# Weight matrices laid out tile by tile in HBM, in a two-block network of 256 tokens

## The chip, the cores and the metric

The kernel runs on one core of a Trainium2 chip. Its time is the device time of one execution in microseconds (us); lower is better. Everything is float32. Weights and inputs lie in HBM (the chip's memory) and reach SBUF (the core's working memory, 128 partitions) by DMA, over 16 DMA engines that all queues of the core share. The kernel's host part is numpy code that arranges the inputs as HBM tensors; it runs before the launch and is not in the time.

## The reference

256 tokens of width 1024 go through two blocks, each of two layers.

```python
# first block, layer i (i = 0: SSD mixer, i = 1: pooling mixer); m, mc come from ada_w, ada_b
x = x + 0.5 * m[:, 2] * swiglu(modulate(x, ...), ffn_w_gate[i, 0], ffn_w_up[i, 0], ffn_w_down[i, 0])
h = h + 0.5 * mc[2] * swiglu(modulate(h, ...), ...)          # context, layer 0 alone
x = x + m[:, 5] * mixer(u, uc)[0]
x = x + 0.5 * m[:, 8] * swiglu(modulate(x, ...), ffn_w_gate[i, 1], ffn_w_up[i, 1], ffn_w_down[i, 1])

# second block, layer l
proj = h @ w_in                                  # attention, short convolution, spatial gating
x = x + g1 * (merged @ w_out)
q = (t @ w_pq).reshape(T, 8, 2, 128)             # expert layer, 8 heads
s = einsum('thpk,hpnk->thpn', q, sub_keys)       # top 16 of 128, twice; then top 16 of 256 pairs
act = gelu(einsum('td,thkd->thk', t, expert_down[experts]))
x = x + g2 * einsum('thk,thkd->td', softmax(best) * act, expert_up[experts])
```

Each token picks 8 x 16 = 128 of 16384 experts, each with a row of 1024 numbers in `expert_down` and one in `expert_up`.

## The kernel before, in words

Each engine has its own instruction stream, written by hand and kept in step by semaphores; each stream runs in order. In the profile PE is TensorE, DVE VectorE, ACT ScalarE, POOL GpSimd and SP the engine that only issues DMAs.

**Weights.** SP loads the weights one tile of 128 x 2048 numbers (1 MB) after another into a ring in SBUF: `wring` with 6 slots in the first block (`load`, line 522), `wring2` with 4 slots in the second (`load2`, line 587); the profile calls both `wring`. A load waits until the tile that had its slot is used up (`weights_consumed`, `weights2_used`). The source is a view of the weight matrix as it came. A gate or up tile takes, for each partition, 8 rows of 256 columns, so 8 pieces of 1 KB (`rows_of(w)[:, :, 256 * i:256 * i + 256]`); `w_in2`, `w_out2`, `peer_wq` and `ssd_w_in` tiles are the same. A down tile or an `ada_w0` tile takes 2 pieces of 4 KB, an `ssd_w_out` tile 16 pieces of 512 B, a `keys` tile (a quarter of a tile) one piece of 2 KB.

**First block.** Five feed-forward parts (`ffn0` to `ffn4`) of 33 tiles each. Each matrix product is made of three passes over a high and a low part of the weights; ACT makes the high part of a tile (`whigh`), DVE the low one (`wlow`). Beside them POOL loads `ada_t` tiles (line 2215, 2 pieces of 4 KB a partition, 3 slots), which DVE multiplies and sums in `condition` (line 1574); there are 112 of them. At the very start 8 tiles of `ada_w0` are multiplied on PE, and DVE turns to their result (line 1458) only behind the low parts of the first three `ffn0` tiles, since it works in order.

**Second block.** It goes through 4 units (2 layers x 2 halves of 128 tokens). A unit has a `mix` (attention, convolution, gating, then the choice of experts) and 128 picks. For pick k POOL gathers, for each of the 128 partitions (tokens), one row of 8 KB (down and up together): 1 MB in all, into one of 8 slots (`rows`, line 2254). DVE multiplies it with the token (line 2125), ACT applies the gelu and makes a diagonal matrix, and PE or DVE adds the up half; then the slot is free. The `mix` of unit u + 1 is woven into the picks of unit u, on each engine at fixed places:

```python
for k in range(PICKS):
    if k >= 2:
        sum_pick(PICKS * unit + k - 2)
    work.go(k)
```

`go(k)` issues those pieces of the mix whose place has come. On PE the 8 `w_in` tiles stand at places 4 to 18, the 4 `w_out` tiles at 35 to 41, the 8 `wq` tiles (`peer_wq`) and 4 `keys` tiles at 48 to 66. So a unit with a mix moves 128 gathers, 20 weight tiles and 4 keys tiles. The mix of unit 0 runs alone, before any pick; unit 3 has no mix beside it. PE waits for its weights in order: while it waits for a tile, its picks wait too.

Of the kernel before, what the change touches and what calls it, by code (L numbers as in the profile page):

```python
# [12 lines left out]
P = 128  # L13
D = 1024
KB = D // P
T = 256
# [3 lines left out]
FFN_ITERS = F // 256  # L20
FFN_TILES = 3 * FFN_ITERS
HIGH_RING = 3
RING = 6
# [14 lines left out]
PH, TOPK, KEYS = 8, 16, 128  # L38
# [31 lines left out]
def consumed(stage, i):  # L70

    return BASE[stage] + i + 1
# [6 lines left out]
ADA_RING = 3  # L79
# [19 lines left out]
RING2 = 4  # L99
# [25 lines left out]
def program(nc, A):  # L125
    ctx = ExitStack()
    with ctx:
        starts = {}

        def sb(name, shape, dt=F32):  # L130
            starts[name] = -(-nc.sbuf_base // 32) * 32
            return ctx.enter_context(nc.sbuf_tensor(name, shape, dt))
# [34 lines left out]
        wring = sb("wring", [P, RING, TILE])  # L167
# [36 lines left out]
        aring = at(2048, ADA_RING, 2, D)  # L204
# [72 lines left out]
        wring2 = second("wring2", [P, RING2, TILE], "wring", 0, RING * TILE)  # L277
# [17 lines left out]
        rows = second("rows", [P, SLOTS, 2 * D], "arena", 3072, AREA)  # L295
# [23 lines left out]
        weights_in = [sem(f"weights_in{i}") for i in range(RING)]  # L319
# [72 lines left out]
        weights2_in = [sem(f"weights2_in{i}") for i in range(RING2)]  # L392
# [119 lines left out]
        @block.sync  # L512
        def _(sp):
            loaded = [0]

            def load(src, a, b):

                n = loaded[0]
                loaded[0] += 1
                if n >= RING:  # L520
                    sp.wait_ge(weights_consumed, n - RING + 1)
                sp.dma_start(wring[:, n % RING, 0:a * b].rearrange("p (a b) -> p a b", a=a), src) \
                    .then_inc(weights_in[n % RING], 16)

            def rows_of(w):
                return w.rearrange("(k p) n -> p k n", p=P)

            def load_columns(w, count, width=256):
                v = rows_of(w)
                for i in range(count):  # L530
                    load(v[:, :, i * width:(i + 1) * width], v.shape[1], width)

            def load_ffn(n, l, f):
                gate_w, up_w, down_w = (rows_of(A[k][l, f]) for k in ("ffn_w_gate", "ffn_w_up", "ffn_w_down"))
                load(gate_w[:, :, 0:256], KB, 256)
                load(up_w[:, :, 0:256], KB, 256)

                load(gate_w[:, :, 256:512], KB, 256)
                load(up_w[:, :, 256:512], KB, 256)
                load(down_w[:, 0:2, :], 2, D)  # L540
                load(gate_w[:, :, 512:768], KB, 256)
                load(up_w[:, :, 512:768], KB, 256)
                load(down_w[:, 2:4, :], 2, D)
                first = loaded[0]
                with sp.Fori(0, (FFN_ITERS - 3) // 2, 1) as it:
                    for j in range(6):
                        slot = (first + j) % RING
                        sp.wait_ge(weights_consumed, it * 6 + (first + j - RING + 1))
                        if j % 3 < 2:
                            src = (gate_w, up_w)[j % 3][:, :, bass.ds(it * 512 + 256 * (3 + j // 3), 256)]  # L550
                            dst = wring[:, slot, :].rearrange("p (a b) -> p a b", a=KB)
                        else:
                            src = down_w[:, bass.ds(it * 4 + 2 * (2 + j // 3), 2), :]
                            dst = wring[:, slot, :].rearrange("p (a b) -> p a b", a=2)
                        sp.dma_start(dst, src).then_inc(weights_in[slot], 16)
                loaded[0] += 6 * ((FFN_ITERS - 3) // 2)
                load(down_w[:, 2 * FFN_ITERS - 2:2 * FFN_ITERS, :], 2, D)

            sp.dma_start(cols[:], A["cols"]).then_inc(cols_in, 16)
            for group in range(2):  # L560
                for i in range(4):
                    load(rows_of(A["ada_w0"])[:, 2 * i:2 * i + 2, group * D:(group + 1) * D], 2, D)
            load_ffn(0, 0, 0)
            load_ffn(1, 0, 0)
            w_ssd = rows_of(A["ssd_w_in"])
            for lat in range(2):
                load(w_ssd[:, :, 5120:5184], KB, 64)
                for i in range(12 if lat else 10):
                    load(w_ssd[:, :, 2048 + 256 * i:2304 + 256 * i], KB, 256)
                for i in range(8 if lat else 0):  # L570
                    load(w_ssd[:, :, 256 * i:256 * i + 256], KB, 256)
            load_columns(A["ssd_w_out"], 8, 128)
            load_ffn(2, 0, 1)
            load_ffn(3, 1, 0)
            load(A["pool_w"].rearrange("g (k p) n -> p (g k) n", p=P), 8, 256)
            load_ffn(4, 1, 1)
            loaded2 = [0]

            def load2(src, a, b):
# [7 lines left out]
                sp.dma_start(wring2[:, n % RING2, 0:a * b].rearrange("p (a b) -> p a b", a=a), src) \  # L587
                    .then_inc(weights2_in[n % RING2], 16)

            for l in range(2):  # L590
                for t in range(TT):
                    for i in W_IN_ORDER:
                        load2(rows_of(A["w_in2"][l])[:, :, 256 * i:256 * i + 256], KB, 256)
                    for i in range(4):
                        load2(rows_of(A["w_out2"][l])[:, :, 256 * i:256 * i + 256], KB, 256)
# [12 lines left out]
            sp.wait_ge(out_stored, 32)  # L608
# [1568 lines left out]
        def _(pool):  # L2177
            g = nc.gpsimd
# [21 lines left out]
            ada = A["ada_t"].rearrange("(b p) k -> p b k", p=P)  # L2200
# [19 lines left out]
            for b in range(NCH * (H // 4) * 2):  # L2220
                c, jb = b // 16, (b // 2) % 8
# [111 lines left out]
```

## Time and profile before

| what | value |
|---|---|
| time, median of 3 runs (lowest to highest) | 3289.71 us (3287.55 to 3296.17) |
| the profiled execution: its own time, its span | 3296.72 us, 3294.7 us |
| PE busy, DVE busy, ACT busy | 80%, 67%, 31% |
| moved by DMA over the span | 976.51 MB in 374436 packets, 260245 of them under 2 KB |
| POOL's queue (q0) | 104848 packets, 656.51 MB |
| SP's queue (q1) | 268304 packets, 312.26 MB |

A packet here is one contiguous piece of a transfer. The span is one execution, from its first to its last instruction; all positions in it are us from its start. The first block ends near 1606 us, the first gather is issued at 1767 us. Units 0, 1 and 2 take their first step behind the opening norm of the mix beside them at 1820.5, 2212.5 and 2605 us; from 2977 us on only picks of unit 3 are left. Times of a wait are idle times of the waiting engine.

### The profile page before, as it was taken

Reading aid. Unit: us, or ns where it says so; the run is one execution under the profiler, and the core shown is the slowest. Engines: PE = TensorE matmul, PEld = TensorE weight load, DVE = VectorE, ACT = ScalarE, POOL = GpSimd, SP = SyncE. Lnnn points to the kernel's source line nnn. Section 1 sums busy time; section 2 is a strip of 40 time slices with the busy share of each in tenths; the row PEclk is TensorE's granted clock in tenths of the full one; section 3 lists DMA queues with packets and bytes.
Section 4 is the critical chain, followed back from the end, with each engine's and each line's share of the span. In section 5 each row is a group of like instructions: output and inputs, shape, how many; then the busy total and the mean of one; then the engine's idle time right before and its main releaser. Section 6 shows DMA issues by size and latency. Waiting matters only on the chain.

```text
span 3294.7 us, 37141 instructions
## 1 busy us (share of the span) xinstructions
PE 2631.4 (80%) x13830; PEld 1990.1 (60%) x13830; DVE 2216.3 (67%) x3855; ACT 1021.6 (31%) x2144; POOL 771.3 (23%) x679
## 2 busy tenths in 40 slices
PE   7999998897699999599873877767766777765566
PEld 4999986686589899599762544235532444321122
DVE  3886865638448868858418666876568765887755
ACT  3433422113134343234322332234222332321222
POOL 0000100004101001001001343443334433445543
PEclk9999998998899999899876989888888888997898
DMA  7777952340159969469536999999999999999998
GB/s 269 271 236 266 367 173 80 105 143 9 39 200 328 333 238 363 146 218 363 184 120 224 401 412 368 417 408 402 405 370 420 402 370 382 398 421 422 422 422 339
DMA packets 374436, 976.51 MB, mean 296 GB/s; under 512 B 17549, under 2 KB 260245, under 8 KB 308256
## 3 DMA queue, kind: packets, MB, share of 16 engines
q0 software_dynamic: 104848, 656.51, 49.5%
q1 hardware_dynamic: 268304, 312.26, 28.7%
q10 hardware_dynamic: 1152, 6.04, 0.5%
q8 instruction: 75, 1.23, 0.2%
q14 instruction: 57, 0.47, 0.0%
HBM read 973.69 MB, written 1.06 MB: 296 GB/s over the span
## 4 chain that ended last, share of the span: by engine, by line
PE 51%; DMA 26%; DVE 13%; ACT 4%; issue 4%; POOL 0%; DVEq 0%; SPq 0%; another core or an unknown queue 0%; ACTq 0%; POOLq 0%
PE psum L624 50%; DMA rows<-in_peer,eidx 17%; DMA wring<-in_peer_wq 4%; DMA wring<-in_w_in 3%; DVE arena L1438 2%; DMA wring<-in_keys 2%; DVE arena L1574 1%; DVE yacc L1441 1%; DVE wlow L1438 1%; PE psum L627 1%; ACT L1060 1%; DVE arena L1444 1%; DVE arena L1441 1%; DVE rows L2125 1%; ACT u L1060 1%
## 5 line engine op out<-in xcount | busy, mean ns | idle before, releaser
L624 PE MATMUL psum<-rows,diag 128*128 128x512 f32 x1392 | 765.9, 693 | 353.5 <-ACT diag L1060 347.5
L2254 POOL DMA_INDIRECT rows<-in_peer,eidx x512 | 636.9, 1244 | 1011.4 <-PE psum L624 665.6
L2125 DVE CUSTOM_DVE_ANT_0 rows<-rows,h2tok 128x1024 f32<-128x1024 f32 x512 | 625.2, 1224 | 282.9 <-DMA rows<-in_peer,eidx 275.7
L624 PEld LDWEIGHTS psum<-rows,diag 128*128 128x128 f32 x1392 | 283.7, 217 | 768.2 <-ACT diag L1060 489.1
L624 PE MATMUL psum<-u_hi,whigh 128*128 128x256 f32 x1760 | 504.3, 287 | 17.7 <-DVE u_lo L1441 14.3
L624 PE MATMUL psum<-u_lo,whigh 128*128 128x256 f32 x1760 | 500.9, 285 | 0.0
L624 PE MATMUL psum<-u_hi,wlow 128*128 128x256 f32 x1760 | 500.8, 285 | 0.0
L1438 DVE TENSOR_TENSOR wlow<-wring,whigh 128x2048 fp32r<-128x2048 f32 x165 | 376.8, 2288 | 164.1 <-ACT whigh L1060 158.0
L1060 ACT ACTIVATE whigh<-wring 128x2048 fp32r<-128x2048 f32 x165 | 314.0, 1908 | 211.8 <-PE psum L624 133.8
L624 PEld LDWEIGHTS psum<-u_hi,whigh 128*128 128x128 f32 x1760 | 340.3, 193 | 21.3 <-issue 15.0
L624 PEld LDWEIGHTS psum<-u_lo,whigh 128*128 128x128 f32 x1760 | 340.9, 194 | 0.0
L624 PEld LDWEIGHTS psum<-u_hi,wlow 128*128 128x128 f32 x1760 | 340.8, 194 | 0.0
L2215 POOL DMA_DIRECT2D arena<-in_ada_t x112 | 80.2, 716 | 1047.0 <-DVE stage L1574 646.6
L624 PE MATMUL psum<-wring,u 128*128 128x256 f32 x1024 | 251.1, 403 | 77.6 <-DMA wring<-in_peer_wq 39.6
L624 PEld LDWEIGHTS psum<-wring,u 128*128 128x128 f32 x1024 | 206.9, 204 | 136.1 <-issue 72.5
L1060 ACT ACTIVATE dots<-dots 128x2 f32<-128x2 f32 x256 | 52.0, 203 | 732.9 <-DVE dots L2125 732.7
L1574 DVE CUSTOM_DVE_ANT_0 arena<-arena 128x1024 f32<-128x1024 f32 x224 | 265.2, 1218 | 10.4 <-DMA arena<-in_ada_t 10.4
L624 PE MATMUL psum<-hid_hi,whigh 128*128 128x256 f32 x880 | 249.3, 283 | 4.7 <-DVE wlow L1438 4.7
L624 PE MATMUL psum<-hid_hi,wlow 128*128 128x256 f32 x880 | 249.0, 283 | 0.0
L624 PE MATMUL psum<-hid_lo,whigh 128*128 128x256 f32 x880 | 249.0, 283 | 0.0
L624 PE MATMUL psum<-u,wring 128*128 128x256 f32 (+1 forms) x992 | 218.9, 382 | 8.4 <-ACT u L1060 7.5
L1441 DVE SCALAR_TENSOR_TENSOR yacc<-rows,dots,yacc 128x1024 f32<-128x1024 f32 x160 | 204.9, 1280 | 28.7 <-ACT dots L1060 28.7
(265 smaller groups left out, 3223.8 us busy)
## 6 DMA issues: line engine op xcount, KB each, us to landing
arena<-in_ada_t POOLq DMA_DIRECT2D x112, 1024.0 KB, 7.4
wring<-in_ffn_w_gate SPq DMA_DIRECT2D x55, 1024.0 KB, 7.1
wring<-in_ffn_w_up SPq DMA_DIRECT2D x55, 1024.0 KB, 7.5
wring<-in_ffn_w_down SPq DMA_DIRECT2D x55, 1024.0 KB, 6.7
wring<-in_w_in SPq DMA_DIRECT2D x32, 1024.0 KB, 19.0
wring<-in_peer_wq SPq DMA_DIRECT2D x32, 1024.0 KB, 16.5
wring<-in_ssd_w_in SPq DMA_DIRECT2D x30, 1024.0 KB, 5.4
wring<-in_w_out SPq DMA_DIRECT2D x16, 1024.0 KB, 19.9
```

The source lines that it names most:

```text
L624: return nc.tensor.matmul(out, lhsT, rhs, start=start, stop=stop, skip_group_check=shared)
L627: return nc.tensor.transpose(out, in_, ident[0:in_.shape[0], 0:in_.shape[0]])
L1060: return nc.scalar.activation(out, in_, fn, **kw)
L1438: return v.tensor_tensor(out, a, b, op)
L1441: return v.scalar_tensor_tensor(out=out, in0=a, scalar=s, in1=b, op0=op0, op1=op1)
L1444: return v.tensor_scalar(out, a, s1, s2, op0, op1) if op1 is not None else v.tensor_scalar(out, a, s1, None, op0)
L1574: ins = v.tensor_tensor_reduce(out=w, in0=w, in1=crow[:, ADA_VECTOR[n], :], scale=1.0, scalar=0.0, op0=ALU.mult, op1=ALU.add, accum_out=st ...
L2125: v.tensor_tensor_reduce(out=rows[:, n % SLOTS, 0:D], in0=rows[:, n % SLOTS, 0:D], in1=h2tok[:, t, :], scale=1.0, scalar=0.0, op0=ALU.mult ...
L2215: pool.dma_start(aring[:, a % ADA_RING], ada[:, 2 * it + 8 * (group + a):2 * it + 8 * (group + a) + 2, :]) \
L2254: pool.indirect_dma_start(out=rows[:, n % SLOTS, :], out_offset=None, in_=A[f"peer{u // 2}"], in_offset=bass.IndirectOffsetOnAxis(ap=eidx[ ...
```

## The change

numpy now writes every weight matrix tile by tile in the order in which the ring takes it, so that a tile is [128, 2048] numbers in HBM with the 8 KB of a partition in one piece, and the whole tile one contiguous megabyte. `load` and `load2` take such a tile as it is; `load_ffn`'s loop picks one by its index. The same holds for POOL's `ada_t` tiles. Each tile in SBUF holds the same numbers at the same places as before, and the number, the order and the queues of the DMAs, all waits and all other engines' instructions stay as they are; the expert tables and the gathers are not touched. A `keys` tile has one piece of 2 KB for each partition before and after.

```diff
-            def load(src, a, b):
+            def load(src):
                 n = loaded[0]
                 loaded[0] += 1
                 if n >= RING:
                     sp.wait_ge(weights_consumed, n - RING + 1)
-                sp.dma_start(wring[:, n % RING, 0:a * b].rearrange("p (a b) -> p a b", a=a), src) \
-                    .then_inc(weights_in[n % RING], 16)
+                sp.dma_start(wring[:, n % RING, 0:src.shape[1]], src).then_inc(weights_in[n % RING], 16)
...
-                load(gate_w[:, :, 0:256], KB, 256)
-                load(up_w[:, :, 0:256], KB, 256)
+                load(gate_w[0])
+                load(up_w[0])
...
-                load(down_w[:, 0:2, :], 2, D)
+                load(down_w[0])
...
-                        load2(rows_of(A["w_in2"][l])[:, :, 256 * i:256 * i + 256], KB, 256)
+                        load2(A["w_in2"][l, i])
...
-                            load2(rows_of(A["peer_wq"][l])[:, :, 256 * head:256 * head + 256], KB, 256)
+                            load2(A["peer_wq"][l, head])
...
-                            load2(A[f"keys{l}"][:, 4 * pair:4 * pair + 4, :], 4, KEYS)
+                            load2(A["keys"][l, pair])
...
-                        pool.dma_start(aring[:, a % ADA_RING], ada[:, 2 * it + 8 * (group + a):2 * it + 8 * (group + a) + 2, :]) \
+                        pool.dma_start(aring[:, a % ADA_RING].rearrange("p a b -> p (a b)"), A["ada_t"][it + 4 * (group + a)]) \
                             .then_inc(ada_in[a], 16)
...
+    def tiles(w, rows, width):
+        lead, (k, n) = w.shape[:-2], w.shape[-2:]
+        w = w.reshape(lead + (k // (rows * P), rows, P, n // width, width))
+        m = len(lead)
+        w = w.transpose(tuple(range(m)) + (m + 3, m, m + 2, m + 1, m + 4))
+        return w.reshape(lead + (n // width * (k // (rows * P)), P, rows * width))
...
-        "ffn_w_gate": I["ffn_w_gate"], "ffn_w_up": I["ffn_w_up"], "ffn_w_down": I["ffn_w_down"],
+        "ffn_w_gate": tiles(I["ffn_w_gate"], KB, 256), "ffn_w_up": tiles(I["ffn_w_up"], KB, 256), "ffn_w_down": tiles(I["ffn_w_down"], 2, D),
...
-        "w_in2": I["w_in_2"], "w_out2": I["w_out_2"], "peer_wq": I["peer_wq_2"],
+        "w_in2": tiles(I["w_in_2"], KB, 256), "w_out2": tiles(I["w_out_2"], KB, 256), "peer_wq": tiles(I["peer_wq_2"], KB, 256),
```

## Rows read from the trace of the kernel before

**Rows 1.** The page: DMA busy tenths and GB/s in 40 slices

```profile
DMA  7777952340159969469536999999999999999998
GB/s 269 271 236 266 367 173 80 105 143 9 39 200 328 333 238 363 146 218 363 184 120 224 401 412 368 417 408 402 405 370 420 402 370 382 398 421 422 422 422 339
```

**Rows 2.** Windows: PE, PEld, DVE, ACT, POOL busy us; clock, DMA share, GB/s

```profile
61.00:447.00 386.00, 383.60 (x3169) 382.90 (x3169) 298.80 (x354) 153.17 (x123) 25.94 (x36) 1.00 0.80 274
...
1820.50:2212.50 392.00, 293.31 (x868) 162.50 (x868) 278.64 (x572) 126.19 (x405) 158.83 (x128) 0.88 1.01 402
2212.50:2605.00 392.50, 286.27 (x840) 158.92 (x840) 277.22 (x573) 124.37 (x405) 152.20 (x129) 0.87 1.01 399
2605.00:2977.00 372.00, 278.52 (x835) 154.47 (x836) 266.05 (x555) 114.00 (x375) 152.08 (x124) 0.90 1.00 394
3020.00:3240.00 220.00, 142.38 (x241) 50.87 (x240) 141.49 (x205) 47.95 (x193) 117.00 (x89) 0.84 1.01 422
```

**Rows 3.** Chain that ended last, unit 0: start us, us, what

```profile
1824.30 25.02 DMA wring<-in_w_in
...
1927.87 36.22 DMA wring<-in_peer_wq
1964.09 19.96 DMA wring<-in_keys
...
1990.07 15.03 DMA wring<-in_keys
...
2013.19 7.33 PE psum L624 x28
```

**Rows 4.** Waits of the whole span: us in total, times, longest

```profile
PE psum L624 <- DMA wring<-in_peer_wq: 39.6, 6, 13.6
...
PE psum L624 <- DMA wring<-in_w_in: 31.2, 4, 14.1
...
PE psum L624 <- DMA wring<-in_keys: 21.7, 4, 9.9
...
DVE arena L1574 <- DMA arena<-in_ada_t: 10.4, 3, 4.7
```

**Rows 5.** DMA queues from 2448 to 2488: packets, MB, share

```profile
q0 software_dynamic: 1998, 14.56, 88.3%
q1 hardware_dynamic: 1875, 1.89, 13.9%
```

**Rows 6.** Windows, columns as in group 2: three short stretches of units 0 and 1

```profile
2248.00:2256.00 8.00, 8.00 (x31) 5.54 (x30) 4.78 (x8) 3.66 (x10) 2.71 (x3) 1.00 1.12 358
2004.00:2020.00 16.00, 14.77 (x53) 10.27 (x54) 8.34 (x21) 3.45 (x13) 3.05 (x3) 0.84 0.77 259
2396.00:2416.00 20.00, 19.19 (x67) 12.68 (x68) 9.14 (x25) 5.65 (x21) 3.81 (x4) 0.86 0.77 253
```

**Rows 7.** DMA from 0 to 40, ScalarE's queue: packets, MB, share

```profile
q10 hardware_dynamic: 720, 3.68, 22.4%
```

**Rows 8.** DMA of units 0, 1, 2; q1 is shown for units 0 and 2

```profile
DMA packets 40061, 157.53 MB, mean 402 GB/s; under 512 B 2455, under 2 KB 22935, under 8 KB 23575
...
q1 hardware_dynamic: 21376, 22.02, 16.9%
DMA packets 39867, 156.72 MB, mean 399 GB/s; under 512 B 2440, under 2 KB 22920, under 8 KB 23432
DMA packets 34892, 146.54 MB, mean 394 GB/s; under 512 B 2275, under 2 KB 18659, under 8 KB 19204
...
q1 hardware_dynamic: 17249, 17.96, 14.6%
```

**Rows 9.** Chain that ended last, at the start

```profile
33.30 11.38 DMA wring<-in_ffn_w_gate
...
48.93 1.12 DVE arena L1458
```

**Rows 10.** Timeline: start us, us, engine, line, operation; PE's ada tiles

```profile
22.81 20.76 PE L624 MATMUL psum<-wring,silu_c 128*2 128x512 f32 x48 [1.49 <-DMA wring<-in_ada_w]
```

More of the change, by code:

```diff
@@ L521, in load @@
                     sp.wait_ge(weights_consumed, n - RING + 1)
-                sp.dma_start(wring[:, n % RING, 0:a * b].rearrange("p (a b) -> p a b", a=a), src) \
-                    .then_inc(weights_in[n % RING], 16)
[L525 to L531, printed above, removed]
-            def load_ffn(n, l, f):
-                gate_w, up_w, down_w = (rows_of(A[k][l, f]) for k in ("ffn_w_gate", "ffn_w_up", "ffn_w_down"))
-                load(gate_w[:, :, 0:256], KB, 256)
-                load(up_w[:, :, 0:256], KB, 256)
-                load(gate_w[:, :, 256:512], KB, 256)
-                load(up_w[:, :, 256:512], KB, 256)
-                load(down_w[:, 0:2, :], 2, D)
-                load(gate_w[:, :, 512:768], KB, 256)
-                load(up_w[:, :, 512:768], KB, 256)
-                load(down_w[:, 2:4, :], 2, D)
+                sp.dma_start(wring[:, n % RING, 0:src.shape[1]], src).then_inc(weights_in[n % RING], 16)
+            def load_ffn(n, l, f):
+                gate_w, up_w, down_w = (A[k][l, f] for k in ("ffn_w_gate", "ffn_w_up", "ffn_w_down"))
+                load(gate_w[0])
+                load(up_w[0])
+                load(gate_w[1])
+                load(up_w[1])
+                load(down_w[0])
+                load(gate_w[2])
+                load(up_w[2])
+                load(down_w[1])
                 first = loaded[0]
@@ L548, in load_ffn @@
                         sp.wait_ge(weights_consumed, it * 6 + (first + j - RING + 1))
[L549 to L555, printed above, removed]
+                        src = (gate_w, up_w, down_w)[j % 3][bass.ds(it * 2 + (3 + j // 3 if j % 3 < 2 else 2 + j // 3), 1)]
+                        sp.dma_start(wring[:, slot, :], src.rearrange("a p n -> (a p) n")).then_inc(weights_in[slot], 16)
                 loaded[0] += 6 * ((FFN_ITERS - 3) // 2)
-                load(down_w[:, 2 * FFN_ITERS - 2:2 * FFN_ITERS, :], 2, D)
+                load(down_w[FFN_ITERS - 1])
             sp.dma_start(cols[:], A["cols"]).then_inc(cols_in, 16)
@@ L561, in _, with load2 @@
                 for i in range(4):
-                    load(rows_of(A["ada_w0"])[:, 2 * i:2 * i + 2, group * D:(group + 1) * D], 2, D)
+                    load(A["ada_w0"][4 * group + i])
             load_ffn(0, 0, 0)
             load_ffn(1, 0, 0)
-            w_ssd = rows_of(A["ssd_w_in"])
             for lat in range(2):
-                load(w_ssd[:, :, 5120:5184], KB, 64)
+                load(A["ssd_w_dt"])
                 for i in range(12 if lat else 10):
-                    load(w_ssd[:, :, 2048 + 256 * i:2304 + 256 * i], KB, 256)
+                    load(A["ssd_w_in"][8 + i])
                 for i in range(8 if lat else 0):
-                    load(w_ssd[:, :, 256 * i:256 * i + 256], KB, 256)
-            load_columns(A["ssd_w_out"], 8, 128)
+                    load(A["ssd_w_in"][i])
+            for i in range(8):
+                load(A["ssd_w_out"][i])
             load_ffn(2, 0, 1)
             load_ffn(3, 1, 0)
-            load(A["pool_w"].rearrange("g (k p) n -> p (g k) n", p=P), 8, 256)
+            load(A["pool_w"])
             load_ffn(4, 1, 1)
             loaded2 = [0]
-            def load2(src, a, b):
+            def load2(src):
                 n = loaded2[0]
@@ L586, in load2 @@
                     sp.wait_ge(weights_consumed, max(i for i in range(FIRST_TILES) if i % RING == n) + 1)
-                sp.dma_start(wring2[:, n % RING2, 0:a * b].rearrange("p (a b) -> p a b", a=a), src) \
-                    .then_inc(weights2_in[n % RING2], 16)
+                sp.dma_start(wring2[:, n % RING2, 0:src.shape[1]], src).then_inc(weights2_in[n % RING2], 16)
             for l in range(2):
@@ L592, in _ @@
                     for i in W_IN_ORDER:
-                        load2(rows_of(A["w_in2"][l])[:, :, 256 * i:256 * i + 256], KB, 256)
+                        load2(A["w_in2"][l, i])
                     for i in range(4):
-                        load2(rows_of(A["w_out2"][l])[:, :, 256 * i:256 * i + 256], KB, 256)
+                        load2(A["w_out2"][l, i])
                     head, pair = 0, 0
@@ L2198, in _ @@
                             allow_small_or_imprecise_dtypes=True))
-            ada = A["ada_t"].rearrange("(b p) k -> p b k", p=P)
             def conditioning(n):
@@ L2307, in blocks @@
         return np.ascontiguousarray(a[0].T.reshape(KB, P, T).transpose(1, 0, 2))
+    def tiles(w, rows, width):
[4 more added lines that the diff above has]
+        return w.reshape(lead + (n // width * (k // (rows * P)), P, rows * width))
+    ada_rows = np.concatenate([I["ada_w"][0].T, I["ada_w"][1].T, I["w_ada_2"][0].T, I["w_ada_2"][1].T])
     arrays = {
         "xT": blocks(I["x"]), "hT": blocks(I["ctx"]), "cols": np.ascontiguousarray(cols),
-        "ada_w0": I["ada_w"][0][:, 0:2 * D], "c_rows": np.concatenate([I["c"].reshape(1, D), I["c_ctx"].reshape(1, D), I["c_2"].reshape(1, D)]),
-        "ada_t": np.concatenate([I["ada_w"][0].T, I["ada_w"][1].T, I["w_ada_2"][0].T, I["w_ada_2"][1].T]),
-        "ffn_w_gate": I["ffn_w_gate"], "ffn_w_up": I["ffn_w_up"], "ffn_w_down": I["ffn_w_down"],
-        "ssd_w_in": I["ssd_w_in"][0], "ssd_w_out": I["ssd_w_out"][0], "pool_w": I["pool_w"][0],
-        "w_in2": I["w_in_2"], "w_out2": I["w_out_2"], "peer_wq": I["peer_wq_2"],
+        "ada_w0": tiles(I["ada_w"][0][:, 0:2 * D], 2, D), "c_rows": np.concatenate([I["c"].reshape(1, D), I["c_ctx"].reshape(1, D), I["c_2"].reshape(1, D)]),
+        "ada_t": tiles(ada_rows, 2, D),
+        "ffn_w_gate": tiles(I["ffn_w_gate"], KB, 256), "ffn_w_up": tiles(I["ffn_w_up"], KB, 256), "ffn_w_down": tiles(I["ffn_w_down"], 2, D),
+        "ssd_w_in": tiles(I["ssd_w_in"][0][:, 0:5120], KB, 256), "ssd_w_dt": tiles(I["ssd_w_in"][0][:, 5120:5184], KB, 64)[0],
+        "ssd_w_out": tiles(I["ssd_w_out"][0], 16, 128), "pool_w": tiles(I["pool_w"][0].reshape(D, T), KB, T)[0],
+        "w_in2": tiles(I["w_in_2"], KB, 256), "w_out2": tiles(I["w_out_2"], KB, 256), "peer_wq": tiles(I["peer_wq_2"], KB, 256),
+        "keys": I["peer_sub_keys_2"].reshape(2, 4, 4, KEYS, P).transpose(0, 1, 4, 2, 3).reshape(2, 4, P, 4 * KEYS),
         "rcnt": rcnt, "bias_onehot": onehot, "rel_bias": rel, "sink": np.ascontiguousarray(I["attn_sink_2"].reshape(2, HEADS // 2, 2).transpose(0, 2, 1).reshape(2, HEADS)),
@@ L2320 @@
     for l in range(2):
-        arrays[f"keys{l}"] = np.ascontiguousarray(I["peer_sub_keys_2"][l].reshape(16, KEYS, P).transpose(2, 0, 1))
         arrays[f"peer{l}"] = np.concatenate([I["peer_down_2"][l], I["peer_up_2"][l]], axis=1)
```

## The prediction

> **What bounds the kernel now.** I began with the page's 40 slices [rows 1]. They fall in two parts. Up to about 1600 us the DMA comes and goes (9 to 367 GB/s); from the slice near 1810 us on it is busy in nine tenths or more of nearly every slice. The windows say what bounds each part [rows 2]. From 61 to 447 us (two feed-forward parts) PE is busy 383.60 of 386.00 us at full clock: a faster transfer buys nothing there. In the last unit, which has no mix beside it (3020 to 3240 us), all traffic is gathers in pieces of 8 KB: 422 GB/s with the DMA share at 1.01, PE busy 142 of 220 us. This is what the transfers can do here. Units 0, 1 and 2, with weight tiles between the gathers, reach 402, 399 and 394 GB/s. So the second block is bound by DMA, and the question is what its bytes would take at 422 GB/s.
>
> Next I read the chain of waits in unit 0 [rows 3]. It leads through weight tiles that land late: 25 us for w_in, 36 us for peer_wq, then 20 and 15 us for keys, although a tile needs only 1.0486 MB / 422 GB/s = 2.5 us. The list of waits has the cost on PE: 39.6 + 31.2 + 21.7 = 92.5 us idle for these three, over the whole span [rows 4]. The queues say why they are late: between 2448 and 2488 us SP's queue moved 1.89 MB in 1875 packets beside 14.56 MB of POOL's queue [rows 5]. That is 1 KB for every 8 KB: the DMA engines give each queue one packet in turn, and the weights' packets are an eighth as large.
>
> By the Trainium skill ("DMA: Bandwidth & Descriptors", Queues, rings and completion order) an engine takes turns between queues by packets, typically of 9 to 17 descriptors. The turns agree with rows 5; so many 1 KB pieces in one turn would have given the weights half the traffic or more, and they have an eighth.
>
> **The change, part by part.** Nothing is added or taken on any engine; what changes is the length of the pieces. Four effects:
>
> 1. *Cheaper bytes in units 0 to 2.* In rows 5 the rate is (14.56 + 1.89) / 40 us = 411 GB/s. For one of 16 engines a turn of 8192 + 1024 B takes 9216 x 16 / 411e3 = 0.359 us; 8192 B at 422 GB/s take 0.311 us. The 1 KB packet costs 0.048 us, and a tile has 64 per engine: 3.07 us against 2.49 us in pieces of 8 KB, so 0.58 us saved. From below: in the 8 us with hardly any gather (2248 to 2256 us) the rate was 358 GB/s [rows 6], 2.93 us a tile, 0.44 us saved. SP's queue moved 22.02 MB in unit 0, as much in unit 1 and 17.96 MB in unit 2 [rows 8]; less 3.1 MB of keys, whose pieces stay, that is 58.9 MB or 56 tiles. Gain 25 to 32 us. I take 31, since most tiles travel between gathers as in rows 5. That SP's kind of queue carries large pieces at that speed is seen at the start: ScalarE's queue moved 3.68 MB in 22.4% of 40 us, 411 GB/s [rows 7].
>
> 2. *Fewer holes in units 0 to 2.* The bytes of the three units (157.53, 156.72, 146.54 MB [rows 8]) need 373.3 + 371.4 + 347.2 = 1091.9 us at 422 GB/s; they took 392.0 + 392.5 + 372.0 = 1156.5. Of the 64.6 us lost, 31 are effect 1 and 34 are holes. Two of them are seen in rows 6: 2004 to 2020 us at 259 GB/s and 2396 to 2416 us at 253, which lose 6.2 and 8.0 us. Each comes right behind the late keys [rows 3]: PE, held up until then, works without a pause (19.19 of 20 us), a step of one wq tile and two picks takes 7.33 us, and the gathers, which have run eight picks ahead, can only follow PE. With pieces of 8 KB a waiting weight tile gets every second turn: it lands in some 2 x 2.5 us plus what is before it in its queue, not in 15 to 36. PE then goes through the mix at the places planned for it. But 7.33 us of PE for a step stand against 2 gathers and at most one tile, 3 x 2.49 = 7.5 us of DMA, so at places 48 to 66 PE is nearly as tight as the DMA, and holes can stay there. From below nothing is regained, from above all 34. I take the middle, 17: the cause of the holes' depth goes, the tightness of that stage does not.
>
> 3. *The start.* DVE reaches the first block's modulation (line 1458) at 48.93 us, because a gate tile asked for at 33.30 us lands 11.38 us later, and ACT and DVE then need 4.2 us to split it [rows 9]. PE has worked off the ada tiles at 22.81 + 20.76 = 43.6 us [rows 10], so at most 48.9 - 43.6 = 5.3 us are to be had, and nothing if the tile lands no sooner. Up to and with that tile 8 ada and 3 feed-forward tiles and ScalarE's 3.7 MB [rows 7] are moved, some 15.5 MB: at 422 GB/s from 2.2 us on they have landed at 39 us, not 44.7, and 4.2 us later DVE is free. I take 4.5.
>
> 4. *ada_t in ffn2.* DVE waits 10.4 us in all for POOL's tiles, three times [rows 4]. Pieces grow from 4 to 8 KB, but those of the weights from 1 to 8, so POOL's queue falls from four fifths to half of the turns' bytes. Bounds 0 and 10.4; I take 2.
>
> The rest is covered: the other loads of the feed-forward and SSD parts land behind PE's work (rows 2, first line); if that cover were missing, each of the 165 feed-forward tiles would be worth up to 0.6 us.
>
> Sum: 31 + 17 + 4.5 + 2 = 54.5 us. From the profiled execution's own 3296.7 us that gives 3242.2; that execution lies 7.0 us above the median of 3289.7, so against the median I predict 3235 us, 1.7% faster.
>
> **The rivals.**
>
> *Cheaper bytes alone.* The holes are PE's own, and the start is not shortened: gain 25 to 31, time 3259 to 3265. For it speaks that PE needs 7.33 of every 7.5 us in the stage with the holes. Chance 0.24.
>
> *All holes close.* Gain 64.6 + 5.3 + 10.4 = 80, time 3209. For it: PE is busy just 293 of 392 us in unit 0 [rows 2]. Chance 0.15.
>
> *No gain.* The length of pieces does not count from 1 KB up, and a weight tile that comes sooner only pushes gathers back. The Trainium skill (the same page, Specifications) sets the least transfer for full rate at 512 B, and by that effect 1 is zero. The rows speak against it: 358 and 411 GB/s with 1 KB pieces, 422 with 8 KB. If the 422 were due to other things (fewer queues at work), the time would stay at 3290, within 10. Chance 0.07.
>
> *Slower: bursts of weights starve the picks.* Four slots come free close together at w_in, w_out and wq. With half the turns, 4 tiles take 20 us, in which 4 gathers land and not 8. POOL has eight slots, so DVE gets its rows up to 10 us later. DVE and PE run the mix behind those picks, so the mix is late too. Nine bursts of 10 us would cost 90 us, less the 54 of the sum: 3326. It decides from the point where POOL has fewer than a few gathers under way, so that the DMA falls idle behind a burst; as long as it stays busy, bytes are only reordered. PE's and DVE's idle quarter [rows 2] speaks against it. Chance 0.05.
>
> My own case, with part of the holes closed, has 0.49.
>
> **How the numbers follow.** The range must take in the case with cheap bytes alone and that with all holes closed: 3207 to 3266 holds 0.88 by these chances; it cannot be drawn tighter without giving up one of the two. A measurement can tell some 0.3% (10 us) from no change. All cases that gain lie beyond that: faster 0.87; same 0.08; slower 0.05.
>
> **What the profile after would show.** SP's queue: 292 tiles with 128 pieces each and some 45000 packets in place of 268304. Windows of units 0 to 2 at 412 GB/s or more. Weight tiles of the second block landing in 5 to 12 us, not 16 to 36, and PE's 92.5 us of waits for them below 30. Units of about 376 us from step to step, not 392. The first DVE instruction of line 1458 near 44 us. The feed-forward parts unchanged. The prediction would be wrong if the rate in unit 3 and in the mixed units differ as before (then pieces are not the cause), or if the holes at places 48 to 66 stay or deepen, or if the DMA falls idle behind bursts while DVE waits for rows.

## The result, and the profile after

| | before | after |
|---|---|---|
| time, median of 4 runs each (lowest to highest) | 3291.43 us (3287.55 to 3296.17) | 3245.36 us (3242.28 to 3246.15) |
| the profiled execution: its own time, its span | 3296.72 us, 3294.7 us | 3242.28 us, 3240.4 us |

After takes 0.9858 of the time of before [0.9841, 0.9875]: 1.4% faster, 46 us. Between the two profiled executions it is 54.4 us.

The page of after, with the same two rows of 40 slices as [rows 1], then packets, queues (packets, MB, share of the 16 engines) and DMA issues (count, KB, median us from issue to landing):

```profile
DMA  7766942240058859549545799999999999999998
GB/s 285 267 236 264 366 177 95 94 143 25 20 200 325 357 207 355 196 171 356 220 148 225 318 406 420 421 421 412 421 420 420 396 409 419 421 421 420 419 422 335
DMA packets 136868, 976.51 MB, mean 301 GB/s; under 512 B 15501, under 2 KB 15509, under 8 KB 18976
...
q0 software_dynamic: 90512, 656.51, 49.8%
q1 hardware_dynamic: 45072, 312.26, 25.3%
...
wring<-in_w_in SPq DMA_DIRECT2D x32, 1024.0 KB, 9.1
wring<-in_peer_wq SPq DMA_DIRECT2D x32, 1024.0 KB, 9.1
...
wring<-in_w_out SPq DMA_DIRECT2D x16, 1024.0 KB, 9.1
```

The bytes are the same to the last digit, in 136868 packets and not 374436; SP's queue has 45072, as forecast. On the right half of the GB/s row 368 to 420 (before, units 0 to 2) has become 396 to 421, with 420 or 421 in most slices. The tiles of the second block land in 9.1 us; before, the page had 19.0, 16.5 and 19.9 for the three.

Windows of after, columns as in [rows 2]: units 0, 1 and 2 from step to step, then the 16 us behind the last `keys` tiles of unit 0, 8 us at the end of unit 0, and unit 3 alone:

```profile
1814.50:2193.00 378.50, 291.62 (x868) 160.16 (x868) 278.83 (x572) 125.76 (x405) 153.82 (x129) 0.90 1.01 416
2193.00:2569.00 376.00, 289.80 (x841) 157.57 (x841) 277.43 (x572) 123.37 (x406) 154.09 (x129) 0.88 1.01 416
2569.00:2937.00 368.00, 289.45 (x847) 157.13 (x848) 276.88 (x569) 115.78 (x386) 154.23 (x129) 0.90 1.01 417
...
1982.00:1998.00 16.00, 16.00 (x61) 10.88 (x62) 9.83 (x40) 4.84 (x19) 4.82 (x4) 0.89 1.02 419
2184.00:2192.00 8.00, 7.80 (x32) 4.42 (x31) 5.48 (x8) 3.34 (x11) 2.65 (x2) 0.79 0.85 329
2980.00:3200.00 220.00, 142.16 (x248) 50.55 (x246) 139.10 (x202) 48.28 (x195) 112.06 (x88) 0.85 1.01 421
```

Read the last column. The mixed units have gone from 402, 399 and 394 GB/s to 416, 416 and 417, while unit 3, whose pieces did not change, stands at 421 (422 before): the units lost time for their weights' pieces, not for anything that the gathers have by themselves. PE's and DVE's busy times are those of [rows 2] within 4 us in units 0 and 1; in unit 2 they are 11 us longer, and the window of after takes in more of the work there (847 matmuls and 569 DVE instructions against 835 and 555). Behind the last `keys` tiles PE works without a pause (16.00 of 16.00 us), as it nearly did before in the stretch with 259 GB/s (14.77 of 16.00 us [rows 6]); the DMA share there is now 1.02 and not 0.77, at 419 GB/s. A hole is left at the seam from unit 0 to unit 1, 329 GB/s with a DMA share of 0.85.

Waits of after over the span (us in total, times, longest):

```profile
DVE rows L2111 <- DMA rows<-in_peer,eidx: 360.0, 278, 3.6
...
DVE arena L1560 <- DMA arena<-in_ada_t: 8.3, 3, 3.5
...
PE psum L610 <- DMA wring<-in_keys: 2.2, 1, 2.2
```

The last is the only wait of PE for weights that is left: 92.5 us [rows 4] have become 2.2. DVE now waits longer for its gathers, 360.0 us where it was 275.7. That is no loss: these units are bound by DMA, so DVE has to be idle somewhere, and it is now at the gathers, which come at full rate. The chain that ended last in unit 0 shows the same (start us, us, what):

```profile
1925.18 18.25 DMA rows<-in_peer,eidx
...
1973.21 8.63 DMA wring<-in_keys
1981.98 7.55 PE psum L610 x24
1989.75 7.34 PE psum L610 x28
```

Of the four late weight tiles of [rows 3], with 96 us of the chain, one is left with 8.63 us. And at the start:

```profile
31.94 9.51 DMA wring<-in_ffn_w_gate
41.48 1.92 ACT whigh L1046
43.42 2.29 DVE wlow L1424
45.71 2.27 DVE arena L1444 x2
```

Line 1444 is line 1458 of before: 45.71 us in place of 48.93 [rows 9].

By place in the program the two traces differ as follows (start of the first instruction of each stage on the chain, before less after): first feed-forward part 3.2 us; end of the second 3.2; the norm of the SSD mixer (line 1818 of before) 5.7; third feed-forward part 5.9; fourth 8.9; first step of unit 0 6.0; end 54.3. So between these two traces 48.3 us come from units 0 to 3, 3.2 from the start, 3.0 from the third feed-forward part (`ada_t` is loaded beside it), and 2.9 are given back at the seam between the blocks, where the chain of before (first fence) and of after (second) read:

```profile
1613.26 0.29 issue
...
1614.66 2.92 DMA arena<-in_rel_bias
```

```profile
1604.52 1.89 issue
...
1607.48 4.26 DMA arena<-in_rel_bias
```

A tiny load on which PE waits starts 1.6 us later behind DVE's last norm and takes 1.3 us longer. Both come with the new layout of the first block: it is so in all three traces that have it (after, its second trace and e7 below: 1.89 us of issue, 4.08 to 4.26 us of load), while in the ten traces with the old layout this load takes 2.92 to 3.42 us or isn't on the chain at all.

The 6.0 us before unit 0 need the other traces beside them, for the first profile of before is the odd one. Its ACT reaches the opening step of unit 0 (`u`, just ahead of PE's first `w_in` product) at 1817.60 us; in the nine other traces with the old first block it is there at 1811.62 to 1814.19 us (mean 1812.8), and in the three with the new one at 1811.57, 1812.20 and 1814.23 us (mean 1812.7). What the new layout wins in the first block is there at its start in all three traces (line 1458 or its like at 45.3 to 45.8 us, not 48.3 to 49.4), but nothing is to be seen of it any more when unit 0 begins. The same holds for the third feed-forward part: from the norm of the SSD mixer to the fourth part it takes 287.2 to 288.0 us with the new layout and 288.0 to 290.3 with the old, so most of the 3.0 us is within what one layout varies by.

### The profile page after: what moved, and what is told of

Its sections match the earlier page's. It is cut to its first block, busy times and chain, and to the rows that moved or that the text cites. A ratio compares the mean times of both kernels' runs of the same rounds, so it can differ in the third digit from the quotient of the medians.

```text
span 3240.4 us, 37121 instructions
## 1 busy us (share of the span) xinstructions
PE 2631.2 (81%) x13830; PEld 1983.2 (61%) x13830; DVE 2218.0 (68%) x3855; ACT 1019.2 (31%) x2144; POOL 738.4 (23%) x679
## 2 busy tenths in 40 slices
DMA packets 136868, 976.51 MB, mean 301 GB/s; under 512 B 15501, under 2 KB 15509, under 8 KB 18976
## 3 DMA queue, kind: packets, MB, share of 16 engines
q1 hardware_dynamic: 45072, 312.26, 25.3%
## 4 chain that ended last, share of the span: by engine, by line
PE 48%; DMA 27%; DVE 15%; ACT 5%; issue 5%; POOL 1%; DVEq 0%; ACTq 0%; POOLq 0%
PE psum L610 48%; DMA rows<-in_peer,eidx 26%; DVE arena L1424 2%; DVE yacc L1427 2%; DVE arena L1560 1%; DVE wlow L1424 1%; DVE rows L2111 1%; PE psum L613 1%; ACT L1046 1%; DVE arena L1430 1%; DVE arena L1427 1%; ACT u L1046 1%; DMA wring<-in_keys 1%; POOL rows L2238 0%; ACT dots L1046 0%
## 5 line engine op out<-in xcount | busy, mean ns | idle before, releaser
L610 PE MATMUL psum<-rows,diag 128*128 128x512 f32 x1392 | 784.1, 706 | 390.8 <-ACT diag L1046 384.3
L2238 POOL DMA_INDIRECT rows<-in_peer,eidx x512 | 624.7, 1220 | 975.4 <-PE psum L610 556.5
L2199 POOL DMA_DIRECT2D arena<-in_ada_t x112 | 59.4, 532 | 1060.6 <-DVE stage L1560 672.2
L610 PE MATMUL psum<-wring,u 128*128 128x256 f32 x1024 | 238.7, 389 | 6.8 <-ACT u L1046 6.8
L610 PEld LDWEIGHTS psum<-wring,u 128*128 128x128 f32 x1024 | 200.3, 197 | 60.0 <-issue 24.7
L610 PEld LDWEIGHTS psum<-u,wring 128*128 128x128 f32 (+1 forms) x992 | 187.1, 189 | 39.1 <-ACT u L1046 7.9
```

The costliest lines, as they stand in the source:

```text
L610: return nc.tensor.matmul(out, lhsT, rhs, start=start, stop=stop, skip_group_check=shared)
L2199: pool.dma_start(aring[:, a % ADA_RING].rearrange("p a b -> p (a b)"), A["ada_t"][it + 4 * (group + a)]) \
L2238: pool.indirect_dma_start(out=rows[:, n % SLOTS, :], out_offset=None, in_=A[f"peer{u // 2}"], in_offset=bass.IndirectOffsetOnAxis(ap=eidx[ ...
```

## The experiments

All kernels below move the same bytes in the same DMAs. For each I divided the second block into windows of 8 us, from 1824 us to 35 us before the end, and worked out the time lost against 422 GB/s in each, 8 x (1 - GB/s / 422). Windows with a DMA share below 0.985 are *holes*; what the others lose is the price of *dearer bytes*. These are the prediction's effects 2 and 1. "Late weights" is PE's idle time for `w_in`, `peer_wq` and `keys` in the list of waits.

| kernel (pieces of the second block) | median us, ratio [95%] | span | lost | holes | dearer bytes | late weights |
|---|---|---|---|---|---|---|
| before (1 KB) | 3291.43 | 3294.7 | 64.5 | 30.6 | 34.0 | 92.5 |
| before again | 3286.82, one run | 3284.8 | 59.0 | 23.6 | 35.4 | 82.8 |
| e2 (1 KB, tile contiguous) | 3291.64, 1.0002 [0.9985, 1.0018] | 3295.3 | 68.1 | 35.3 | 32.8 | 94.6 |
| e3 (2 KB) | 3288.62, 0.9993 [0.9979, 1.0007] | 3286.8 | 60.3 | 46.1 | 14.2 | 82.4 |
| e4 (4 KB) | 3250.74, 0.9878 [0.9857, 0.99] | 3247.4 | 22.5 | 13.6 | 8.9 | 20.9 |
| e1 (8 KB) | 3249.16, 0.988 [0.986, 0.9901] | 3244.3 | 18.8 | 13.6 | 5.3 | 0 |
| e5 (`wq` 8 KB, rest 1) | 3263.28, 0.9924 [0.9905, 0.9942] | 3259.0 | 32.5 | 6.9 | 25.6 | 27.8 |
| e6 (`w_in`, `w_out` 8 KB, `wq` 1) | 3275.51, 0.9957 [0.994, 0.9974] | 3265.7 | 37.3 | 17.3 | 19.9 | 46.1 |
| e9 (`wq` 8 KB, rest 2) | 3260.15, 0.9909 [0.9889, 0.993] | 3258.0 | 31.5 | 17.1 | 14.4 | 32.5 |
| e10 (`wq` 2 KB, rest 8) | 3273.0, 0.9942 [0.992, 0.9965] | 3270.8 | 43.8 | 32.5 | 11.4 | 44.1 |
| e7 (first block 8 KB, second 1) | 3286.7, 0.9987 [0.9974, 1.0001] | 3282.1 | 54.9 | 17.8 | 37.1 | 78.6 |
| after (8 KB, both blocks) | 3245.36, 0.9858 [0.9841, 0.9875] | 3240.4 | 15.7 | 9.9 | 5.7 | 2.2 |
| e8 (after again) | 3247.74, 0.9869 [0.9844, 0.9893] | 3247.0 | 17.8 | 12.3 | 5.5 | 0.8 |

A row of the table beyond the median is one execution. That of before lies 5.3 us above its median and that of e2 5.6 above, that of e6 lies 7.9 below; the others are within 3.2 us of theirs. How much the columns vary by themselves is seen in the four rows whose second block has 1 KB pieces throughout (before, before again, e2, e7): 17.8 to 35.3 us of holes, 32.8 to 37.1 us of dearer bytes, 78.6 to 94.6 us of late weights.

My theory was that the weights' pieces are dear by themselves and, since the DMA engines give each queue a packet in turn, make the weights late. The rivals: that the gain is only that of cheaper bytes; that it is HBM's address order (a whole tile is now one megabyte in one piece) and not the piece; that it comes from the first block.

**e1_second_8k**: the second block's weights alone, in 8 KB pieces; the first block, `ada_t` and `keys` as before.

```diff
-                        load2(rows_of(A["peer_wq"][l])[:, :, 256 * head:256 * head + 256], KB, 256)
+                        load2(A["peer_wq"][l, head].rearrange("a p n -> p a n"), PIECES, TILE // PIECES)
...
+    def pieces(w):
+        t = tiles(w, KB, 256)
+        return t.reshape(t.shape[:2] + (P, PIECES, TILE // PIECES)).transpose(0, 1, 3, 2, 4)
...
-        "w_in2": I["w_in_2"], "w_out2": I["w_out_2"], "peer_wq": I["peer_wq_2"],
+        "w_in2": pieces(I["w_in_2"]), "w_out2": pieces(I["w_out_2"]), "peer_wq": pieces(I["peer_wq_2"]),
```

`w_in2` and `w_out2` are loaded in the same way; `PIECES` is 1.

> The kernel before, with the tile layout for the second block's three matrices alone (w_in2, w_out2, peer_wq; pieces of 8 KB); the first block's weights and ada_t as before. My theory: the gain sits in units 0 to 2, so this gives 42 to 48 us less than before (about 3246), and the start and ffn2 stay as before. Rival, that the first block gives a good part (15 us or more): 3255 or more.

41.6 us less than before's median on the same chip (3290.72 in 18 runs), just short of the 42 to 48 that I expected. The second block has nearly the whole gain.

**e2_whole_tile_1k**: `PIECES = 8`. A tile is one contiguous megabyte in HBM, but each piece of a partition is 1 KB as before.

> As the run of the second block alone, but each tile, still one contiguous megabyte of HBM, is ordered so that a partition's part comes in 8 pieces of 1 KB, 128 KB apart. My theory, that the length of a piece counts: as before, 3291 within 6, w_in landing in about 25 us. Rival, that the order of the addresses in HBM counts (whole tiles from one place): 3245, as with 8 KB pieces.

Ratio 1.0002: nothing. The address range is that of e1, the number and length of the pieces that of before, and so is the time: that a tile is one contiguous megabyte is refuted as the cause. What counts is the length of one partition's piece. A piece is two things at once, one packet and one stretch of HBM; 1 KB packets that read a partition's 8 KB one behind the other were not tried, so for the price of the bytes the two are not told apart. For the turns of the queues it is the packet that counts, as the fences below show.

**e5_wq_8k and e6_win_wout_8k**: e1 for `peer_wq` alone, and for `w_in2` and `w_out2` alone.

> Pieces of 8 KB for peer_wq alone, 24 of the 56 tiles that travel beside the gathers; w_in2 and w_out2 stay at 1 KB. Theory of two effects (cheaper bytes and a larger share of the turns, which ends the holes behind the late keys): 24 x 0.55 = 13 us for the bytes and 13 to 17 us for the holes, 26 to 30 us in all, time 3261 to 3265, no hole below 300 GB/s at places 48 to 66. Rival, cheaper bytes alone and all gain in proportion to the tiles: 24/56 of some 46 us = 20 us, time 3271, holes as before.

> Pieces of 8 KB for w_in2 and w_out2 alone (32 of the 56 tiles); peer_wq stays at 1 KB. Two effects: 32 x 0.55 = 18 us for the bytes and little more, since the holes behind the late keys stay (two of 253 to 259 GB/s as before): 18 to 22 us, time 3269 to 3273. Rival, in proportion to the tiles: 32/56 of some 46 us = 26 us, time 3265.

27.4 us for `wq` and 15.2 for the others; together 42.6, e1 has 41.6. e5 is as expected, e6 is a miss: I had expected 18 to 22 us. Of the tiles 24 of `wq` and 32 of the others travel beside gathers, so a `wq` tile gives 1.14 us, more than the 0.58 that its bytes alone could, one of the others 0.48. In e5 the dearer bytes fell by 8.4 us and the holes by 23.7 against the first profile of before, by 16.7 against the second: the late tiles of places 48 to 66 made most of the holes. PE's waits in e5 name what is left:

```profile
PE psum L625 <- DMA wring<-in_w_in: 27.8, 5, 11.3
```

**e3_second_2k and e4_second_4k**: `PIECES = 4` and 2.

> Second block's three matrices alone, in pieces of 2 KB. A packet costs a fixed part of about 0.01 us beside its bytes by the price of the 1 KB pieces, so 2 KB gives back 0.33 of the 0.58 us a tile, 18 us; with turns by packets the weights have a fifth of the traffic and not a ninth, and a tile lands in about 13 us, which closes a part of the holes: 30 to 36 us less than before, time 3255 to 3261. Rival, cheaper bytes alone: 18 us, time 3273.

> Second block's three matrices alone, in pieces of 4 KB. The fixed part of a packet gives back 0.50 of 0.58 us a tile, 27 us; the weights have a third of the traffic, and the holes are closed as with 8 KB: 40 to 45 us less than before, time 3246 to 3251. Rival, cheaper bytes alone: 27 us, time 3264.

4 KB gave what 8 KB gives (ratio 0.9878 and 0.988). 2 KB was a miss: I had expected more than half of the gain and got 2.0 us, which can't be told from nothing. The table says where it went. Dearer bytes fell as forecast, from 34.0 to 14.2, and the holes rose from 30.6 to 46.1. The waits of e3:

```profile
PE psum L625 <- DMA wring<-in_keys: 45.1, 6, 10.5
PE psum L625 <- DMA wring<-in_w_in: 33.3, 8, 6.6
...
PE psum L625 <- DMA wring<-in_peer_wq: 4.0, 3, 2.1
```

PE's wait for weights is 82.4 us, as good as unchanged; it only moved to `keys`, the last tiles of the same stage. Behind it comes the hole, in the windows of e3:

```profile
2008.00:2016.00 8.00, 8.00 (x32) 5.35 (x31) 1.52 (x3) 1.91 (x7) 1.54 (x2) 0.95 0.60 207
2016.00:2024.00 8.00, 8.00 (x32) 5.39 (x32) 5.27 (x17) 2.20 (x8) 2.47 (x3) 1.00 0.82 277
```

PE is busy all 8 us and the DMA 60%. Why that is so at 2 KB and not at 4 is seen in the queues, in 10 us of unit 0 with weight tiles waiting: before, e3, e4 and after (packets, MB, share of the engines; q0 is POOL's, q1 SP's).

```profile
q0 software_dynamic: 500, 3.60, 87.5%
q1 hardware_dynamic: 501, 0.50, 14.5%
```

```profile
q0 software_dynamic: 445, 3.25, 78.9%
q1 hardware_dynamic: 442, 0.88, 23.1%
```

```profile
q0 software_dynamic: 378, 2.70, 65.2%
q1 hardware_dynamic: 378, 1.43, 35.6%
```

```profile
q0 software_dynamic: 297, 2.17, 52.1%
q1 hardware_dynamic: 280, 2.02, 49.0%
```

The packets of the two queues are alike in each, 500 to 501 and 378 to 378 (a few of them are of 4 bytes). Equal counts would also come of equal turns of several packets. The start and the duration of every packet, which the traces hold, settle it. They do not name a packet's engine, but several times more packets start 3 or 4 ns before the end of another than at any other distance, which marks the next one on the same engine. Wherever this names one predecessor it is a packet of the other queue: in the 12 us that end with each of these stretches 811 times of 811 in before, 767 of 767 in e3, 637 of 637 in e4 and 576 of 585 in after. So it is one packet in turn, and a queue's share of the bytes follows from the length of its pieces: 12%, 21%, 35% and 48% for the weights. The Trainium skill ("DMA: Bandwidth & Descriptors", Queues, rings and completion order) has turns by packets, typically of 9 to 17 descriptors; these traces agree with the turns, but each turn holds one piece.

The MB over 10 us give the weights 50, 88, 143 and 202 GB/s while both queues are busy. PE needs, in the stage of places 48 to 66, 8 `wq` and 4 `keys` tiles (9.4 MB) in some ten steps of 7.33 us [rows 3], 128 GB/s. 50 and 88 lie below, 143 and 202 above. How long the stage took is seen at SP, which asks for a tile when PE has done with the one in its slot; unit 0, first `wq` and last `keys` tiles, before (first fence) and after (second; start us, us of issuing):

```profile
1922.70 41.34 SPq L587 DMA_DIRECT2D wring<-in_peer_wq  x4
...
2013.01 1.01 SPq L587 DMA_DIRECT2D wring<-in_keys  x2
```

```profile
1916.80 15.84 SPq L574 DMA_DIRECT2D wring<-in_peer_wq  x4
...
1989.56 0.99 SPq L574 DMA_DIRECT2D wring<-in_keys  x2
```

That is 90.3 us before and 72.8 after. Over units 0, 1 and 2 of all thirteen traces:

| pieces of `wq` | traces | first `wq` to last `keys` tiles, us | mean |
|---|---|---|---|
| 1 KB | before, before again, e2, e6, e7 | 82.1 to 94.5 | 86.7 |
| 2 KB | e3, e10 | 83.7 to 90.8 | 87.9 |
| 4 KB | e4 | 75.6 to 79.1 | 76.8 |
| 8 KB | e1, e5, e9, after, e8 | 70.6 to 75.3 | 72.1 |

So it is a threshold, and it is where the need puts it. Above it the stage goes at PE's own pace. Below it PE is held and the stage is some 15 us longer, but not as long as the share would make it: 9.4 MB at 50 or 88 GB/s would be 189 or 107 us. The reason is that with PE held no slot comes free for a gather, and the weights have the engines nearly to themselves: from 1976 to 1984 us before, SP's queue moved 2.33 MB and POOL's 0.60, from 2000 to 2008 us in e3 2.15 and 0.84. So the stage is as long at 2 KB as at 1 KB, and what the cheaper bytes save there is spent in the hole behind it.

The explanation by need and share was made after e3, so it was put to two further kernels.

**e9_wq_8k_rest_2k and e10_wq_2k_rest_8k**: e3 with 8 KB for `peer_wq` alone, and e1 with 2 KB for `peer_wq` alone.

```diff
-                            load2(A["peer_wq"][l, head].rearrange("a p n -> p a n"), PIECES, TILE // PIECES)
+                            load2(A["peer_wq"][l, head].rearrange("a p n -> p a n"), WQ_PIECES, TILE // WQ_PIECES)
```

> Second block alone: peer_wq in pieces of 8 KB, w_in2 and w_out2 in pieces of 2 KB. Theory formed on the 2 KB run: at places 48 to 66 PE wants about 0.94 MB of weights for each 7.33 us, 128 GB/s; pieces of 2 KB get 90 GB/s beside the gathers, 4 KB 140 GB/s, so what counts for the holes is peer_wq's share alone. Then this gives the 27 us of peer_wq alone and some 0.33 us for each of the 32 other tiles, 10 us: 3253 (3249 to 3258). Rival, that 2 KB pieces do harm wherever they stand: no better than peer_wq alone, 3263 or more.

> The mirror image: peer_wq in pieces of 2 KB, w_in2 and w_out2 in pieces of 8 KB. By the same theory the weights stay short at places 48 to 66 and the holes stay: no better than w_in2 and w_out2 alone (3275), 3270 to 3282, PE waiting for keys. Rival, bytes alone: 24 x 0.33 = 8 us better than w_in2 and w_out2 alone, 3267 or less.

e10 came as the theory has it (3273.0, 16.8 us below before): with 8 KB everywhere but in that one stage, holes are 32.5 us and PE waits as in e3, for `keys`, with the same hole behind.

```profile
PE psum L626 <- DMA wring<-in_keys: 39.6, 5, 9.4
...
PE psum L626 <- DMA wring<-in_peer_wq: 4.5, 2, 3.5
```

```profile
2384.00:2392.00 8.00, 8.00 (x32) 5.38 (x31) 2.04 (x6) 1.91 (x7) 2.05 (x2) 0.97 0.58 201
```

e9 turned the miss of e3 into 29.6 us of gain by the pieces of `wq` alone, which confirms where the loss sat, but it stopped 2 us short of the range that I gave it. PE still waits for `w_in`, as long as in e3:

```profile
PE psum L626 <- DMA wring<-in_w_in: 30.4, 8, 5.6
```

**e7_first_8k**: after, with the second block's three sources put back to those of before; the first block's weights, `ada_t` and `keys` keep the new layout.

> The changed kernel with w_in2, w_out2 and peer_wq put back into their old layout, so the new layout for the first block, ada_t and keys alone. My theory: 3 us at the start, 3 in ffn2 and 3 in the SSD part, less some at the seam of the blocks: 4 to 8 us less than before, time 3283 to 3287. Rival, nothing in the median: within 3 us of before.

3.9 us less than before's median (3290.62), with an interval that ends at 1.0001: small, and not told from nothing by this measurement. With e1's 41.6 us it makes 45.5, the whole change 46 and, measured again, 42.9.

**e8_after_again and e11_before_again**: both kernels unchanged, for the spread and for a second trace of each.

> The changed kernel again, for a closer ratio: 3245 within 3 us, 45 to 48 us below before. If the two profiled executions were typical, the difference would be 54.

> The kernel before, profiled once more, to see how its holes differ from one execution to the next: its 23 runs so far spread over 24 us (3279 to 3303), those of the changed kernel over 7. Theory: the spread sits in the holes of units 0 to 2, so a time away from 3295 shows itself as more or less than the 31 us of holes found in the first profile, with the cost of the bytes the same 34 us.

After again has 3247.74 us, 42.9 below before's median (3290.62) where I had expected 45 to 48. Before ran from 3279.3 to 3302.91 us in the 23 runs beside e3 and e4; after from 3242.28 to 3249.0 in both its measurements. The two profiled executions of before differ by 9.9 us of span. Of these 5.4 are there already at the first step of unit 0; behind it the second one lost 5.5 us less, with 7.0 us less of holes (30.6 and 23.6). That late weights are what makes the time vary is not shown: e3, whose weights are as late (82.4 us), ran from 3284.51 to 3294.02 us in 12 runs, e2 from 3280.52 to 3302.22 in as many.

## Why the prediction was right, and where it was off

- *The bound.* Right. Units with weights reached 416 GB/s from 394 to 402, unit 3 stayed, and PE's and DVE's work did not change.
- *Effect 1, cheaper bytes, 31 us.* 34.0 - 5.7 = 28.3 us. The price of a piece taken from [rows 5] holds over the whole range: a tile of 8 pieces for each partition gives 31 us for seven pieces fewer, so 4/7 of 31 = 18 us at 2 KB and 6/7 = 27 us at 4 KB, and the traces show 19.8 and 25.1. The packets' own durations say the same: in the four stretches with turns above their medians are 46, 84 and 160 ns for 1, 2 and 4 KB and 312 to 316 for 8 KB, which is 5 to 8 ns for each piece beside its bytes; the prediction's working has 48 and 311. Where the 5.7 us lie that are left was not tried; `keys` still has pieces of 2 KB. The rule of the Trainium skill ("DMA: Bandwidth & Descriptors", Specifications) that 512 B is enough for the full rate does not hold here: 411 GB/s with 1 KB pieces beside gathers [rows 5] have become 420 and 421 in most slices.
- *Effect 2, fewer holes, 17 us of 0 to 34.* 30.6 - 9.9 = 20.7 us between the first traces; between the second ones (23.6 and 12.3) it is 11.3. I had taken the middle for want of a measure. The measure would have been the weights' need, 128 GB/s, against their share by turns. With it one sees why the holes of places 48 to 66 and just behind them close altogether (21.5 of the 30.6 us before, none after; 419 GB/s from 1982 to 1998 us), against what I wrote of that stage's tightness. What stays is elsewhere: 5.8 of the 9.9 us at the two seams between units (329 GB/s at 2184 us), of which I had said nothing, and the rest just ahead of the first `wq` tile of units 0 and 2.
- *Effect 3, the start, 4.5 us of 0 to 5.3.* 3.2 us at the start. The gate tile landed at 41.45 us, not 39: the transfers ran at 391 GB/s from 2 to 10 us and at 371 from 10 to 20, not at 422. DVE came 4.3 us behind, as forecast.
- *Effect 4, `ada_t`, 2 us.* 3.0 us over the third feed-forward part between the first traces, though DVE's listed wait fell only from 10.4 to 8.3; over all traces the means of this stretch differ by 1.7. POOL spends 532 ns on issuing such a load, 716 before. Of effects 3 and 4 together nothing is left at the first step of unit 0 (means of 1812.8 and 1812.7 us, without the first profile of before), and in the median they are the 3.9 us of e7, if anything.
- *Nothing is added.* The feed-forward parts are unchanged but for that. The 2.9 us given back at `rel_bias` were not foreseen, and they come with the new layout of the first block.
- *The sum.* 54.5 us forecast, 54.4 measured between the two profiled executions (3242.2 forecast, 3242.28 measured); parts off by -2.7, +3.7, -1.3, +1.0 and -2.9 cancel, together with 2.5 us ahead of the SSD mixer's norm for which nothing in the sum stood. So the exactness is luck, the order is not. It is luck in the choice of traces too: before's was the slower and after's the faster of the two that were profiled, and the other pairings of these four executions differ by 37.8, 44.5 and 47.7 us.
- *Where it was off.* Against the median I predicted 3235 us and it is 3245.36. Median against median the change is worth 46 us, not 54.5. Of the 10 us that are missing, 1.7 are that before's median moved from 3289.71 to 3291.43 with the fourth run. The other 8.4 are the sum's: effects 3 and 4 were forecast at 6.5 us and e7 has 3.9, with an interval that reaches nothing; effects 1 and 2 were forecast at 48 and e1 has 41.6. With 28.7 us for the bytes (34.0 - 5.3) that leaves about 13 for the holes in e1: an estimate, and the term that was off most. Taking 7.0 us off for the profiled execution was not the error. 4.8 us of its offset lie ahead of unit 0, where the sum removes nothing of them, and its units lost 64.5 us where the four traces with 1 KB pieces lost 54.9 to 68.1 (mean 61.6). But these 4.8 us stand in the 54.4 between the two profiled executions as if the change had won them, and after's execution lies 3.1 us below its own median. The range, 3207 to 3266, held the result.
- *An inference that does not follow.* I wrote that turns of 9 to 17 descriptors "would have given the weights half the traffic or more". That holds only if POOL's queue had one piece in its turn; with as many in both, the share is an eighth as well, and rows 5 can't tell the two apart. The packet by packet order can, and it has one in each.
- *Rivals.* "Cheap bytes alone" (3259 to 3265) fell with the time, and with the holes of e5 and after. "All holes close" (3209) did not come: 9.9 us of holes stay, and 5.7 us of dearer bytes. "No gain" (the length of pieces does not count from 1 KB up) fell with the rates and the time; the step to 2 KB shows no gain in time, but its bytes did become 19.8 us cheaper. Of "bursts starve the picks" nothing is seen: DVE's longest wait for a gather is 3.6 us.

## What to carry to other kernels

Where a stream of small pieces shares the DMA engines with one of large pieces, work out two things: what each piece costs beyond its bytes (here 0.046 us for 1 KB on one engine, of which 1024/8192 of 0.312 = 0.039 are its bytes), and what share of the bytes the turns leave to the stream, against what its consumer needs in its tightest stage. The first is linear in the number of pieces and small; the second is a threshold, so the first step (here 2 KB) may give nothing and the next (4 KB) nearly everything. Numpy can lay weights out for one long piece per partition at no cost on the chip, and here 4 KB was enough.

Before a gain is put down to a place by the difference of two traces, lay a third and a fourth beside them. Here 4.8 us of the first block were one execution's own lateness and looked like a gain of the change.

## What the runs showed of the hardware that was not expected

- Pieces of 2 KB gave 2.0 us, pieces of 4 KB 40 us (3290.62 to 3288.62 and to 3250.74), in the same DMAs at the same places.
- Packets of two busy queues alternate one for one, whatever their length: 2215 times of 2215 in the stretches with 1, 2 and 4 KB pieces against 8 KB, 576 of 585 with 8 KB against 8.
- A packet has 5 to 8 ns beside its bytes (46, 84, 160 and 312 to 316 ns for 1, 2, 4 and 8 KB).
- A whole tile as one contiguous megabyte of HBM was worth nothing by itself (1.0002).
- With `wq` in pieces of 1 or 2 KB the stage with the `wq` and `keys` tiles took 82 to 95 us, with 4 KB 76 to 79, with 8 KB 71 to 75, in units 0, 1 and 2 of thirteen traces.
- Left open: why the time of before varies over 24 us in 23 runs and that of e3, with weights as late, over 10 us in 12. And that the holes are deeper at 2 KB (46.1 us in one trace) than at 1 KB (17.8 to 35.3 in four) because an equally long stage has fewer us of bytes in it is argued from the stage's length; no run separates it.
